# Layer-0 weight conversion, the mixer's yield points, and one FFN convolution tap in a two-layer hybrid decoder

## The reference

```python
def conv_ffn(h, w_up, conv_w, w_down):
    gu = causal_dwconv(h @ w_up, conv_w)
    g, u = jnp.split(gu, 2, axis=-1)
    return (jax.nn.silu(g) * u) @ w_down

for i in range(DEPTH):
    h = rmsnorm(x, norm_mix_gain[i])
    z = h @ w_in[i]
    ...
    y_a = rglru_group(a_u, a_gate, ...)
    y_b = hgrn2_group(b_q, b_f, b_v, b_g, ...)
    y_c = shortconv_group(c_b, c_c, c_v, ...)
    y = jnp.concatenate([y_a, y_b, y_c], axis=-1)
    x = x + y @ w_out[i]
    x = x + conv_ffn(rmsnorm(x, norm_ffn_gain[i]), ffn_w_up[i], ffn_conv_w[i], ffn_w_down[i])
    gate = jax.nn.sigmoid(x @ ple_w_gate[i])
    x = x + gate * (p[i] @ ple_w_proj[i])
return rmsnorm(x, final_norm_gain)
```

## Time and profile before

| | us |
|---|---|
| median of 2 runs | 3174.82 (3171.73 to 3177.92) |
| the profiled execution | 3175.14 |
| its span, slowest of 8 cores | 3174.1 (the others from 3156.6) |
| TensorE busy in the span | 2062.4 (65%) |
| VectorE busy | 1539.3 (48%) |
| ScalarE busy | 1417.1 (45%) |
| GpSimd busy | 235.8 (7%) |
| granted TensorE clock, cores | 0.789 to 0.812 |

### The profile page before, as it was taken

How to read it: one execution, slowest core, us unless ns; L and a number is a source line. 1 busy time by engine, 2 the same in 40 slices (tenths; PEclk the granted TensorE clock), 3 DMA queues, 4 the chain that set the end, 5 groups by cost and what they waited for, 6 DMA issues and landing times.

```text
span 3174.1 us, 34187 instructions; the slowest of 8 cores (3156.6 to 3174.1 us)
## 1 busy us (share of the span) xinstructions
PE 2062.4 (65%) x9328; PEld 899.2 (28%) x9328; DVE 1539.3 (48%) x2730; ACT 1417.1 (45%) x2624; POOL 235.8 (7%) x345
## 2 busy tenths in 40 slices
PE   3151684545875557755597758776886778675886
PEld 3020231212332222322242324322332334232333
DVE  1114545514466244563456545654565456635824
ACT  2234354523556234562365526552556345633523
POOL 0110011120121201212000000000000000000000
PEclk9985696766887868988698869977898879786996
DMA  6680397672774836736142213322231314131332
GB/s 189 207 245 0 91 282 229 181 240 100 220 242 127 247 97 193 225 115 207 43 130 92 80 67 107 106 66 87 81 125 51 110 60 133 52 114 47 116 104 106
DMA packets 276394, 421.81 MB, mean 133 GB/s; under 512 B 15888, under 2 KB 197136, under 8 KB 276208
## 3 DMA queue, kind: packets, MB, share of 16 engines
q1 hardware_dynamic: 258224, 362.60, 38.1%
q0 software_dynamic: 17984, 57.03, 4.6%
HBM read 354.16 MB, written 65.40 MB: 132 GB/s over the span
## 4 chain that ended last, share of the span: by engine, by line
PE 34%; DVE 20%; DMA 18%; ACT 15%; issue 10%; POOL 1%; DVEq 1%; SPq 0%; ACTq 0%; POOLq 0%
PE ps_accF L276 19%; PE ps_accM L276 13%; DMA wscr<-sb_cvt 9%; DVE sb_t16F L757 5%; DMA sb_wst<-w_up 3%; ACT L763 2%; ACT sb_t16F L748 2%; DMA sb_io<-p 1%; DVE sb_t16F L753 1%; ACT sb_t16F L763 1%; DVE sb_t32F L819 1%; DVE sb_t32M L566 1%; DMA sb_wst<-w_in 1%; DMA sb_wst<-w_down 1%; DVE sb_hyF L439 1%
## 5 line engine op out<-in xcount | busy, mean ns | idle before, releaser
L276 PE MATMUL ps_accF<-sb_hyF,sb_wbf 128*128 128x512 bf16 x3328 | 885.3, 424 | 143.3 <-ACT sb_t16F L748 112.9
L757 DVE SCALAR_TENSOR_TENSOR sb_t16F<-sb_t16F,sb_par 128x512 bf16<-128x512 bf16 x704 | 542.5, 771 | 74.4 <-DVE sb_t16F L757 1.4
L276 PEld LDWEIGHTS ps_accF<-sb_hyF,sb_wbf 128*128 128x128 bf16 x3328 | 347.5, 106 | 660.3 <-issue 372.9
L276 PE MATMUL ps_accM<-sb_hyM,sb_wbf 128*128 128x512 bf16 x1856 | 463.3, 408 | 72.5 <-ACT sb_t32M L531 16.2
L276 PE MATMUL ps_accF<-sb_a_buf,sb_wbf 128*128 128x512 bf16 x1408 | 343.0, 406 | 34.5 <-ACT sb_t16F L748 17.5
L753 DVE TENSOR_SCALAR sb_t16F<-sb_t16F,sb_par 128x512 bf16<-128x512 bf16 x352 | 131.1, 373 | 353.4 <-ACT sb_t16F L748 348.1
L276 PEld LDWEIGHTS ps_accM<-sb_hyM,sb_wbf 128*128 128x128 bf16 x1856 | 189.6, 103 | 329.1 <-issue 143.3
L748 ACT ACTIVATE sb_t16F<-ps_accF 128x512 bf16<-128x512 f32 x352 | 210.3, 597 | 122.4 <-PE ps_accF L276 99.4
L276 PE MATMUL ps_accM<-sb_t16M,sb_cbf 128*128 128x512 bf16 x64 | 35.3, 551 | 318.1 <-ACT sb_t16M L445 268.3
L276 PEld LDWEIGHTS ps_accF<-sb_a_buf,sb_wbf 128*128 128x128 bf16 x1408 | 144.6, 103 | 229.2 <-issue 89.3
L369 ACT ACTIVATE sb_cvt<-sb_wst 128x1024 bf16<-128x1024 f32 (+2 forms) x64 | 61.8, 966 | 302.0 <-DMA wscr<-sb_cvt 170.7
(11 more groups left out here) (130 smaller groups left out, 2236.0 us busy)
## 6 DMA issues: line engine op xcount, KB each, us to landing
sb_wbf<-wscr SPq DMA_DIRECT2D x344, 512.0 KB, 3.9
wscr<-sb_cvt POOLq DMA_DIRECT2D x204, 256.0 KB, 5.7
sb_wbf<-wscr SPq DMA_DIRECT2D x128, 352.0 KB, 3.5
sb_wst<-w_up SPq DMA_DIRECT2D x66, 512.0 KB, 7.3
sb_wst<-w_in SPq DMA_DIRECT2D x36, 512.0 KB, 6.3
sb_wst<-w_down SPq DMA_DIRECT2D x24, 512.0 KB, 5.7
sb_io<-w_up SPq DMA_DIRECT2D x22, 512.0 KB, 9.2
sb_io<-x SPq DMA_DIRECT2D x16, 512.0 KB, 4.0
```

Source lines behind the costliest of these rows:

```text
L276: S.op("pe", lambda e: e.matmul(out, lhsT, rhs, start=start, stop=stop, skip_group_check=skip), r=r, w=w, signal=signal)
L757: S.op("dve", lambda e, pre=pre, cv=cv, ci=ci, tap=tap: e.scalar_tensor_tensor(out=cv[:, 0:TT], in0=pre[:, tap:tap + TT], scalar=pc(l, "ff ...
```

## The change

Four edits.

1. Layer 0's first 17 conversion groups (w_in, gates, w_out: 33 units) go round seven convert slots instead of two: the two old ones and five pairs of chunks of `a_buf`, which the FFN doesn't use before the first up-projection.
2. `headnorm_to_y` is split: `headnorm_sq` emits the Square at the end of the chain that makes its input; the matmul and the rest come two yields later (short convolution) or three (RG-LRU). In the RG-LRU group the yields between the gates, the square root and the recurrence are gone.
3. In the HGRN2 group the yields between Ln, the scan, the Exps and the products are gone; two yields stand before the transposes and scores, both score matmuls come together, and their products with v follow one yield later. The mixer pass has 54 yields, the FFN's 37 are as before.
4. The first tap of the FFN convolution is a scaled copy on ScalarE, straight from the PSUM bank, instead of a `tensor_scalar` on VectorE from `pre`.

```diff
+    cvt_slots0 = list(cvt_slots)
+    for m in range(6, 11):
+        S.newsem(("cvo", m))
+        cvt_slots0.append((a_buf[:, 2 * m:2 * m + 2, :].rearrange("p a t -> p (a t)"), [a_b[2 * m], a_b[2 * m + 1]], ("cvo", m)))
...
-            cv_t, cv_b, cv_sem = cvt_slots[t % len(cvt_slots)]
+            cl_ = cvt_slots0 if (l == 0 and idx < 17) else cvt_slots
+            cv_t, cv_b, cv_sem = cl_[t % len(cl_)]
...
-    def headnorm_to_y(l, src, srcb, ychunk):
+    def headnorm_sq(src, srcb):
         tq, tqb = t16M.get()
         S.op("act", lambda e: e.activation(out=tq[:, 0:TT], in_=src[:], func=AF.Square), r=[srcb], w=[tqb])
+        return tq, tqb
+
+    def headnorm_to_y(l, src, srcb, ychunk, tq, tqb):
...
-            yield
-            headnorm_to_y(l, u, ub_, 6 + c)
-            yield
+            tq, tqb = headnorm_sq(u, ub_)
+            yield
+            yield
+            headnorm_to_y(l, u, ub_, 6 + c, tq, tqb)
...
-            yield
             S.op("act", lambda e, rt=rt: e.activation(out=rt[:], in_=rt[:], func=AF.Ln, bias=1.0, scale=-1.0),
                  r=[rtb], w=[rtb])
             S.op("act", lambda e, rt=rt: e.activation(out=rt[:], in_=rt[:], func=AF.Exp, scale=0.5),
                  r=[rtb], w=[rtb])
-            yield
...
-            yield
-            headnorm_to_y(l, u, ub_, c)
-            yield
+            tq, tqb = headnorm_sq(u, ub_)
+            yield
+            yield
+            yield
+            headnorm_to_y(l, u, ub_, c, tq, tqb)
...
             G, Gb = t32M.get()
...
-            yield
             S.op("act", lambda e, lf=lf, G=G: e.activation(out=lf[:], in_=G[:], func=AF.Exp), r=[Gb], w=[lfb])
             S.op("act", lambda e, G=G: e.activation(out=G[:], in_=G[:], func=AF.Exp, scale=-1.0), r=[Gb], w=[Gb])
-            yield
...
                 r=[kgb, eGb], w=[kdb])
             yield
+            yield
             ptr, ptr_b = accM.get()
...
-                yield
+            yield
+            for h in range(2):
+                hs = slice(64 * h, 64 * h + 64)
                 for j in range(4):
...
             eGs.append((eGl[:, c, :], eGl_b[c], qg, qgb))
-            yield
...
                 cv, cvb = t16F.get()
-                S.op("dve", lambda e, pre=pre, cv=cv, ci=ci: e.tensor_scalar(
-                    out=cv[:, 0:TT], in0=pre[:, 2:TT + 2], scalar1=pc(l, "ffn_cw", 44 * 2 + ci), scalar2=None,
-                    op0=ALU.mult), r=[preb, par_b[l]], w=[cvb])
+                S.op("act", lambda e, pst=pst, cv=cv, ci=ci: e.activation(
+                    out=cv[:, 0:TT], in_=pst[:], func=AF.Copy, scale=pc(l, "ffn_cw", 44 * 2 + ci)),
+                    r=[pst_b, par_b[l]], w=[cvb])
```

8 lines of the change are left out of this document (4 added, 4 removed).

## The result

The changed kernel takes 3104.5 us (median) against 3171.9 us for the kernel before in the same comparison: a ratio of 0.978, 95% interval 0.975 to 0.981. So it is faster by 2.2%, some 67 us, inside the range of the prediction (2940 to 3185) and on its side, but with half of the 130 us forecast: it lies just outside the band that the forecast itself was given (2990 to 3100), between it and rival B (3140).

The account below looks back on a forecast made before the run. Bound: latency, in-order queues standing behind each other, with TensorE waiting. Terms -15-5-4-38-58-10.5 = -130.5 us from a median of 3174.8 gave about 3045 us (forecast band 2990 to 3100, chance 0.50); range 2940 to 3185.

Parts of the forecast that it names:

- rival B: HGRN2 beside the PLE gate stalls it for as long as the tail shrinks; rounds 1 to 7 give nothing: 3140; chance 0.16.
- Term 1: Seven convert slots for the first 33 units: -15 us in the conversion ahead of everything, -5 for w_out's units.
- packets would slow down as much as overlap wins: Conversion ahead of the mixers: the case in which seven slots gain 0 there, against -19 at the other end.
- Term 2, round 8: FFN alone, tap on ScalarE: step from 4.48 to 3.9 to 4.0 us, 22 steps x -0.48 = -10.5 us.
- Term 2, mixed rounds: Mixer beside FFN: added taps fill ScalarE's wait for VectorE, so +0.2 us a step, not 1.2; first stretch +1.
- rival C: ScalarE bounds the up-projection: each of 154 mixed steps pays 1.2 us instead of 0.2, +154, 3199; chance 0.09.
- Item 3a: Head norms and RG-LRU beside up-projection: bank waits behind an 11.4 us ScalarE block replace Square's wait; -1 plus 1.5 us.
- Item 3c: HGRN2 groups move from the mixer tail beside down-projection and PLE gate: tail -20.5 us, new place +3.5 a round.
- Rounds 1 to 3, -38: Rounds with weight conversion: yields move likewise, conversion stalls are untouched and swallow some: -14, -12, -12 us; ends 0 and -60.
- A: TensorE's wait for Squares is not replaced by bank waits; rounds 1 to 7 each win 21 us more: 2898; chance 0.17.
- D: After 8 to 11 us of idle TensorE may get half its clock longer; 20 us more a round, 3185; chance 0.08.
- E: The seven convert slots bring nothing: 3065, inside the forecast, with no chance of its own.

Follow-up runs that it names:

- no tap: The changed kernel with the FFN tap back on VectorE: ratio 0.974 (0.969 to 0.978), 3081 us.
- p early: The changed kernel with the load of p for a tile's PLE gate emitted ahead of its down-projection instead of behind it: ratio 0.963, 3047 us.
- RG-LRU alone: The kernel before with only the head-norm and RG-LRU yields changed (Square ahead of the yields, one yield a group fewer): ratio 1.0064, 3184 us.

## Why the prediction was right or wrong

**The bound of the kernel: right.** Latency in order on ScalarE and VectorE, with TensorE as the victim; taking a wait or the casts out of ScalarE's queue gained (three experiments), and moving work onto ScalarE lost.

**Term 1, slots, -20: right** (by themselves -22 by the ratio). That round 0 as a whole came out at -22 against -24 is partly luck: in the median core the slots alone took 31 us from it and HGRN2 alone 11, and two experiments that change nothing in round 0 (no tap, p early) have it at 339 to 340 us in the mean, 8 us below the profiled execution of the change. The value of -15 between 0 and -19 for the first stretch was 14 in the trace (the first Square at 122.8 us, before at 136.5). The worry that packets would slow down as much as overlap wins came half true: landing times nearly doubled, and the stretch still shrank.

**Term 2, round 8, -10.5: a size.** It gave 7 to 8 us. The step is 4.09 us and not 3.9 to 4.0: a half takes ScalarE 1.65 us where 1.08 + 0.6 were assumed, but Silu starts 0.25 us later than in line. That is 0.39 us for each of 22 steps, 8.6 us, of which the *up* part of round 8 shows 7.3.

**Term 2, mixed rounds: nearly right in clean rounds.** Laid in a row, the forecast has +0.2 for eleven steps and +1 for the first stretch, 3 us a round; alone the tap cost 4. Steps take 4.09 and 5.4 us where 4.0 and 5.3 were put. The cover it named, VectorE's lateness, did hold: rival C's price of 1.2 a step is excluded. In rounds 1 to 3, whose 66 steps would pay 79 us by it, the *up* parts grew by 6 us with the tap alone and are 17 us (mean of the cores) longer with it than without it in the whole change.

**Item 3a, Square and block: right in kind.** 11.5 us for the block against 11.4, the Square's wait 4.13 against 3.9, the second stretch set by ScalarE's steps, a bank wait where the Square's wait was. The stretch should have grown by 0.5 us and grew by 3.7; 1.1 of the difference lies in the steps (4.09 and 5.4), the rest is open. Of table loads the second stretch of round 5 has 13 instead of 16, where 12 were forecast; the whole of the round has 28 instead of 30. The rows decide between the two prices weighed: a load takes 1283 ns, and the instruction behind it starts 1.29 to 1.30 us after it. The Trainium skill, ScalarE: Activation LUTs, section What ACT_TABLE_LOAD costs, has the same 1283 ns for the load and more for a switch with its drain; no row here shows the drain.

**Item 3c, the tail: right, the new place: wrong.** -20.5 were forecast for the tail and it lost 20.2. Its price beside the gate was set at 3.5 and the down-projection's at 1; together they are 8.0. The step that failed is the price "6 us, where TensorE has about 4 in hand: +2". The 6.3 us were about right, but TensorE had 2.5 in hand (it waited 3.80, where it waited 1.15 for the first sigmoids before), and the matmuls behind the wait took 1.7 us more, at a granted clock of 0.68, in three of the four clean rounds. With 1.0 more for the load of p and 1.1 more in the waits of the PLE product (4.3 against 3.2) that is 6.4 of the 7.1 us by which this stretch grew. The prediction had weighed the clock only as a rival of its own, for the long waits, and not as part of each short one.

**Rounds 1 to 3, -38: wrong.** They gave 5 (10 in the mean of the cores). The step that failed is that conversion stalls "are untouched": the *up* parts grew by 44 us (32 in the mean) where clean rounds grew by 4.5 each, against -61 in the tails. Casts stand in the same queue as the FFN copies, and without them there most of the stall is gone (*up* of 206 to 210 us against 195 in clean rounds of that run); that this is also what made it grow with the change is argued, not shown. The prediction's own table had the stall (107, 66 and 62 us above a clean round) and did not ask on whose queue it lies. This miss is 33 us (28 in the mean), that of the clean rounds 27.

**The rivals.** None came in full. A (the waits vanish) is excluded by the experiment with RG-LRU alone; B (HGRN2 costs the same in the new place) comes to 9.5 of 16.5 us or 12 of 16 with HGRN2 alone, and to 8 of 20 in the change; D's clock shows in the 1.7 us above, but the second stretch has the granted clock 0.81 that it had before. E is excluded by the slots alone.

## What to carry to other kernels

On an in-order engine that frees another's buffers, ask of every instruction what it waits for, not only how long it runs: a cast that waits for a DMA, a Square that waits for a scan and a sigmoid behind a table switch each cost more than their busy time, and the cure was to put them on an idle queue or ahead of a stretch in which that engine has no work. Edits that move such work interact (one gave nothing alone and 6 us a round in company, and in the *up* parts of rounds 1 to 3 it and the tap cost 18 us apart and 32 together, in the mean of the cores), so take one out of the whole as well as one put on the old kernel before a part is judged. And price a stretch by the queue its stall lies on: a regime that seems to belong to something else, as the conversion here, need not hold still while you change its neighbours.

## What the runs showed of the hardware

- A wait of 3.80 us on TensorE was followed by sixteen matmuls in 5.30 us (granted clock 0.68) in round 5 of the changed kernel and by sixteen in 3.61 us (1.00) in round 4; a wait of 11.68 by thirty-two in 9.00 us (0.80). So a short wait can cost 1.7 us more than itself, or nothing more.
- Slow matmuls behind a wait need not be the clock's doing: the first sixteen of the PLE gate took 5.62, 5.63 and 5.83 us at granted clocks of 0.93, 0.73 and 0.71, paced by ScalarE copies of 128x512 that start 0.52 us apart.
- The PSUM copy on ScalarE with a per-partition scale takes 671 ns, the plain one 598.
- With seven convert slots instead of two, a 512 KB load took 9.9 to 11.1 us from issue to landing instead of 5.3 to 5.8, and what was moved from 60 to 140 us still rose from 227 to 256 GB/s.
- A table load on ScalarE takes 1283 ns, and the instruction behind it starts 1.29 to 1.30 us after the load's start.
